# Grouped-query attention: the value products of a head pair issued in three slots in place of five

## The reference, cut to what matters

```
k_all = concatenate([cache_gqa_k, k]); v_all = concatenate([cache_gqa_v, v])
s = einsum('bqkgd,blkd->bkgql', qblk, k) * scale      # 16 heads, 4 of them share a key head
p = softmax(s)
o = einsum('bkgql,blkd->bqkgd', p, v)                 # this product
# layer 3: the latent keys of a query block are its own tile and its neighbours (+-128 tokens),
#          all 128 cached keys beside them, and one sink logit per head
```

## Time and profile before

| | |
|---|---|
| median of 3 runs | 3430.19 us |
| profiled execution | 3428.06 us |
| its span | 3426.3 us |
| TensorE matmul busy | 3130.1 us (91%) |
| VectorE busy | 2160.0 us (63%) |
| ScalarE busy | 1078.0 us (31%) |
| GpSimd busy | 318.6 us (9%) |
| mean granted TensorE clock | 0.943 of full speed |

### The profile page before, as it was taken

The page is one execution under the profiler, slowest core; times in us unless marked ns, Lnnn a source line. Parts: engine busy times, 40 slices in busy tenths (PEclk is TensorE's granted clock), DMA queues, the critical chain, the costliest instruction groups (busy, mean ns, idle before and its releaser), DMA issues.

```text
span 3426.3 us, 54082 instructions
## 1 busy us (share of the span) xinstructions
PE 3130.1 (91%) x21137; PEld 2844.0 (83%) x21137; DVE 2160.0 (63%) x4376; ACT 1078.0 (31%) x2031; POOL 318.6 (9%) x330
## 2 busy tenths in 40 slices
PE   4599999988888999998999889999998789899998
PEld 2499999966568999997775589999996657899998
DVE  5866666666656666665736646666666564666665
ACT  2232222234543222222325423222223463322221
POOL 0000000022310000000317600000002221000000
PEclk6699999989999999998998889999998899999999
DMA  7433323210022332321210033332321001222221
GB/s 290 173 116 118 114 94 118 103 33 27 1 76 97 111 122 93 115 110 54 74 52 6 4 123 121 113 122 88 120 99 39 22 1 63 69 72 71 73 72 43
DMA packets 44624, 292.27 MB, mean 85 GB/s; under 512 B 4944, under 2 KB 8272, under 8 KB 10192
## 3 DMA queue, kind: packets, MB, share of 16 engines
q1 hardware_dynamic: 44496, 290.56, 23.1%
HBM read 286.33 MB, written 4.21 MB: 85 GB/s over the span
## 4 chain that ended last, share of the span: by engine, by line
PE 83%; DVE 9%; issue 4%; ACT 3%; DMA 1%; POOL 0%; SPq 0%; POOLq 0%; DVEq 0%; ACTq 0%
PE psA L1538 37%; PE psB L1538 23%; PE psA L1653 3%; PE psA L1655 3%; PE psA L1654 3%; PE psB L1554 2%; PE psA L737 2%; PE psB L672 1%; PE psB L654 1%; ACT probs L876 1%; DVE top L1164 1%; PE psB L1561 1%; DMA m_stage<-w_mod_dram 1%; PE psB L795 1%; DVE sq_sum L1931 1%
## 5 line engine op out<-in xcount | busy, mean ns | idle before, releaser
L1538 PE MATMUL psA<-h_hi,w_hi 128*128 128x322 f32 x2816 | 655.9, 314 | 13.2 <-DVE h_lo L1971 13.2
L1538 PE MATMUL psA<-h_lo,w_hi 128*128 128x322 f32 x2816 | 652.9, 313 | 0.0
L1538 PE MATMUL psA<-h_hi,w_lo 128*128 128x322 f32 x2816 | 649.2, 312 | 0.0
L1990 DVE SCALAR_TENSOR_TENSOR xT<-psB,mod,xT 128x128 f32<-128x128 f32 x1128 | 425.8, 434 | 258.4 <-PE psB L1538 258.4
L1538 PEld LDWEIGHTS psA<-h_hi,w_hi 128*128 128x128 f32 x2816 | 477.5, 191 | 15.4 <-issue 15.2
L1538 PEld LDWEIGHTS psA<-h_lo,w_hi 128*128 128x128 f32 x2816 | 480.2, 190 | 0.0
L1538 PEld LDWEIGHTS psA<-h_hi,w_lo 128*128 128x128 f32 x2816 | 479.8, 190 | 0.0
L2047 DVE TENSOR_SCALAR conv<-u_raw,vec_sb 128x642 f32<-128x642 f32 x176 | 108.3, 615 | 486.7 <-ACT u_raw L1850 486.7
L1850 ACT ACTIVATE u_raw<-psA 128x644 f32<-128x644 f32 x176 | 124.6, 708 | 761.5 <-PE psA L1538 761.5
L1538 PE MATMUL psB<-g_hi,wo_hi 128*128 128x322 f32 x1408 | 336.3, 321 | 23.7 <-DVE g_lo L2068 23.7
L1896 DVE TENSOR_TENSOR w_lo<-w_stage,w_hi 128x512 fp32r<-128x512 f32 x504 | 321.4, 684 | 29.2 <-ACT w_hi L1764 29.1
(11 more groups left out here) (215 smaller groups left out, 4649.1 us busy)
## 6 DMA issues: line engine op xcount, KB each, us to landing
w_stage<-weights_dram SPq DMA_DIRECT2D x126, 1024.0 KB, 4.8
m_stage<-w_mod_dram SPq DMA_DIRECT2D x96, 1024.0 KB, 7.6
wo_stage<-w_out_dram SPq DMA_DIRECT2D x44, 1024.0 KB, 4.8
xT<-xT_dram SPq DMA_DIRECT2D x1, 2576.0 KB, 16.7
yT_dram<-xT SPq DMA_DIRECT2D x8, 322.0 KB, 2.2
inv_count<-inv_count_dram SPq DMA_DIRECT2D x1, 1280.0 KB, 13.6
rope_raw<-rope_dram SPq DMA_DIRECT2D x3, 256.0 KB, 2.6
k_cache_d<-ck_dram SPq DMA_DIRECT2D x8, 64.0 KB, 2.0
```

Source lines behind the costliest of these rows:

```text
L1538: ins = pe.matmul(o, wp, xp[:, a:b], start=first and n == 0, stop=last and n == 2)
L1990: ins = dve.scalar_tensor_tensor(out=xT[:, d, c:c + w], in0=psB[:, bank, at_:at_ + w], scalar=gate[:, d, i:i + 1], in1=xT[:, d, c:c + w], ...
```

## The change

The table now names tuples of key tiles: the cached tile with tile 1 in the first slot, tiles 2 and 3 two slots later, tile 4 two slots after that. The first and the last slot of a pair are the same as before. `pv` loops over the tiles that it is given; waits, matmuls, their operands and the one semaphore increment at the end are the same. ACT and DVE ask for the last tile of the tuple, and find `out_hi` and `out_lo` in the slot where they were. The new `pv` is one line longer, so L672 is L673 in the changed file, and the lines behind move with it.

```
         for d in range(KT):
-            for i, kt in enumerate((CACHE_TILE, 1, 2, 3, 4)):
-                PV_PARTS[UNIT_AT[2 * d + 1, NT - 1] + 4 + i] = (d, kt)
+            for i, kts in enumerate(((CACHE_TILE, 1), (2, 3), (4,))):
+                PV_PARTS[UNIT_AT[2 * d + 1, NT - 1] + 4 + 2 * i] = (d, kts)
...
-            def pv(d, kt):
-
-                if kt == CACHE_TILE:
+            def pv(d, kts):
+
+                if kts[0] == CACHE_TILE:
                     for h in (2 * d, 2 * d + 1):
                         g_taken(pe, l, "pc", h, 1)
                         g_taken(pe, l, "p", h, NT - 1)
                     if d:
                         pe.wait_ge(s_att[l], d)
-                qs = [j for j in range(1, NT) if kt == CACHE_TILE or l == 1 or kt in band_tiles(j)]
-                x, y = (qs[0] - 1) * P, qs[-1] * P
-                for odd in range(2):
-                    ins = pe.matmul(OUT_LAT[odd * DH:(odd + 1) * DH, x:y], value(kt, 2 * d // GROUP),
-                                    pt[(2 * d + odd) % 4][:, kt - 1, x:y], start=(kt == CACHE_TILE),
-                                    stop=(kt == NT - 1), skip_group_check=True)
-                if kt == NT - 1:
+                for kt in kts:
+                    qs = [j for j in range(1, NT) if kt == CACHE_TILE or l == 1 or kt in band_tiles(j)]
+                    x, y = (qs[0] - 1) * P, qs[-1] * P
+                    for odd in range(2):
+                        ins = pe.matmul(OUT_LAT[odd * DH:(odd + 1) * DH, x:y], value(kt, 2 * d // GROUP),
+                                        pt[(2 * d + odd) % 4][:, kt - 1, x:y], start=(kt == CACHE_TILE),
+                                        stop=(kt == NT - 1), skip_group_check=True)
+                if kts[-1] == NT - 1:
                     ins.then_inc(s_pv[l], 1)
...
-                if s - 1 in PV_PARTS and PV_PARTS[s - 1][1] == NT - 1:
+                if s - 1 in PV_PARTS and PV_PARTS[s - 1][1][-1] == NT - 1:
                     out_hi(PV_PARTS[s - 1][0])
```

## The result

The changed kernel is slower, as forecast: a median of 3446.33 us (3444.27 to 3450.71, 5 runs) against 3429.26 (3428.54 to 3431.15, 5 runs) on the same chip, a ratio of 1.0050 [1.0035, 1.0065]. The medians differ by 17.07 us. Between the profiled executions the difference is 3446.61 - 3428.06 = 18.55 us; the steps of the forecast gave 13.5.

A forecast was written before the change was run, and what follows sets the result against it. The prediction took waits on ACT's copies, released by the previous slot's scores, to bound slots with products. Its terms, 6.9 + 0.9 + 4.3 + 1.4 = 13.5 us, on the median 3430.19 gave 3443.7 us; range 3433 to 3451.

The forecast's parts named there:

- the steps of the forecast: Both attentions: first and second pairs of layers 1 and 3 lose 6.9 + 0.9 + 4.3 + 1.4 = 13.5 us.
- What bounds it: Slots with products: in every second slot TensorE waits for ACT's copy, released by scores issued one slot earlier.
- A product costs 1.19 alone and 0.86 behind another: TensorE's time per key tile in layer 1, in us; merging saves 0.33 us of TensorE's own time each.
- First pairs: Slots 12 to 16 of a group: +1.72 us for each of four in layer 1, +1.07 in layer 3.
- idle before L654: TensorE's wait for ACT's copies in slots 14 and 16: grows from 0.34 and 0.27 us to about 1.5 each.
- Second pairs of layer 1: From slot 20: DVE's work covers most of the delay; about 0.3 us is left each, 0.9 for three.
- The cover: Slot 21, layer 1: transposes already wait 0.77 us for DVE, so slot 20's extra 0.86 us end about there.
- Second pairs of layer 3: DVE covers 0.21 us of slot 20's 0.43; with slot 22's product, 0.45 us each, 1.4 for three.
- rival 4: TensorE's clock falls more often behind new gaps: up to 1.7 us each, six more, 3453.9 us; chance 0.06.
- counter-argument: Against more clock falls: slots without products, 67% busy, kept the full clock at 854 to 862 us.
- Outside the attentions the span was to be unmoved: Only the attentions of layers 1 and 3 end later, by 8 and 6 us; all else is unmoved.

The follow-up runs named there:

- the doubles in odd slots: Against the kernel before: first pairs have the cached tile in slot 12, tiles 1 and 2 in 13, 3 and 4 in 15; median 3432.92 us, ratio 1.0009.
- the doubles in 12 and 15: Against the kernel before: first pairs have the cached tile and tile 1 in slot 12, tiles 2 and 3 in 15, 4 in 16; median 3428.99 us.
- the filled kernel: The changed kernel plus throw-away matmuls of constants in layer 3's thin slots (18, 19 of each group, 61, 62); median 3441.91 us, ratio 1.0036.
- the kernel without tiles 1 and 3: The kernel before, with the products of key tiles 1 and 3 left out for pairs 0 to 6 in layers 1 and 3; 3433.11 us, one execution.
- the repetition: The changed kernel run once more with nothing edited, for a second profile; median 3444.02 us in 4 runs, ratio 1.0047.

## Why the prediction was right

**What bounds it.** Right, and shown: removing tile 1's product changed nothing past one maximum, and removing tile 2's took 0.85 us. But the loop is one of two. Scores issued in slot s release, through maximum, shift and exponential, the copy with which ACT begins its next slot; slot s+1's transposes wait for it, and slot s+1's product stands behind that wait and ahead of the scores of slot s+2. So products of even slots load one loop and those of odd slots another, and the one with more load sets the pace. Before, the even loop held three products, 2 x 0.86 + 1.19 = 2.91 us (two of them share their switch of array halves with the key transposes in slots 12 and 14), the odd one 2 x 1.19 = 2.38. The change put all five, 2.91 + 2 x 0.86 = 4.63, into the even loop: +1.72. The prediction had the first half of this, which is all that the change needed. It said that ACT copies odd tiles only and that the waits stand in even slots alone; ACT also copies the cached keys' transposes, and the wait for those in slot 17 is the odd loop's. The second half cost the prediction nothing here, and made the expectation for the doubles in odd slots wrong by some 13 us: 10 less forecast, 2.8 more measured. The count of products gives the direction of the runs with moved doubles and not their size: by it the doubles in 12 and 15 leave the even loop at 2.91 and would cost nothing, and cost 0.56.

**A product costs 1.19 alone and 0.86 behind another.** Right for its purpose: each merge costs 0.82 or 0.83 us by itself and the two 1.69. The difference of 0.33 us shows again in the product of slot 14, whose removal gave 0.86 back and not 1.19: it has transposes of keys beside it that also use half of the columns, where the prediction took all else to use the full array. That the difference is the price of entering and leaving half of the array is argued from these numbers. The Trainium skill (TensorEngine Tiling (Array Packing), Key Properties) says that a change of mode drains TensorE. The double product's 1.88 us, against 2 x 1.08 for two single ones, agrees; it never reached the sum, since TensorE had that time idle.

**First pairs.** 1.72 forecast, 1.71 to 1.72 measured in layer 1, slot by slot as worked out (slot 13 +0.82, 15 +1.69, 17 +1.69); 1.07 against 1.09 in layer 3. One sign came out differently: idle before L654 grew to 1.54 us in slot 14, as said, but in slot 16 it stayed at 0.27. The new wait on the second key's copy, 1.04 us ahead of slot 16's scores, has taken the time that TensorE would have idled before its transposes.

**Second pairs of layer 1.** 0.3 forecast, 0.49, 0.48 and 0.16 measured, the last one mixed with a fall of the clock elsewhere. The cover was DVE's, as said; 0.2 us less of it than estimated. These rows of the second pair answer to the earlier trace rows:

```profile
867.89 0.66 PE L654 MATMUL psB<-ident_sb,probs 128*128 128x128 f32 x4 [0.33 <-DVE pt L1214]
...
870.21 0.66 PE L654 MATMUL psB<-ident_sb,probs 128*128 128x128 f32 x4 [0.97 <-ACT pt L825]
...
875.29 0.66 PE L654 MATMUL psB<-ident_sb,probs 128*128 128x128 f32 x4 [0.63 <-DVE ptc L1209]
```

Slot 21's wait on DVE is 0.33 us where it was 0.77, slot 22 has a new one of 0.97 us, for ACT, and slot 24 one of 0.63 us for DVE's copy of the context unit, the one that the prediction named.

**Second pairs of layer 3: the term that was off.** "I take 0.45", 1.4 us for three; measured 6.2. The steps themselves cost 0.21 to 0.25 each, half of the estimate, as the filled kernel shows; the other 1.7 to 1.9 us each are the clock, which the sum put at nothing. It falls earlier against the context unit's scores than before, and mostly stays at 1.2 GHz for 6.9 us in place of 3.5. That is rival 4 in kind. Its price holds ("up to 1.7 us" for 3.4 us; falls of that length cost 0.0 to 1.6 here), its places don't. It looked for falls after the new gaps of slots 14 and 16, and the clock is 1.00 there in layer 1; the cost came behind slots that had a fall already. Nor does its counter-argument stand: slots 67% busy kept the full clock in its row, but 5.36 us of 7.30 did not in the kernel without tiles 1 and 3.

The account: layer 1 7.9 us; layer 3 4 x 1.09 + 3 x 0.23 = 5.1 for the steps, which makes 13.0 against 13.5 forecast; and the other 5.5 us of layer 3, the clock's. Together 18.5 of 18.55 measured. Outside the attentions the span was to be unmoved, and it is +1.35 us ahead of layer 1 and -1.15 between the layers: that sign failed, and the two nearly cancel by luck, as the falls in slots 46 and 63 of layer 3 do. So the mechanism and the steps were right, and a term of 5.5 us was missing. The forecast median, 3443.7, lies 2.6 us under the measured one, but part of that closeness is the kernel before, 0.9 us faster here than where the forecast started: between medians the loss is 17.07 us here and 15.62 in the repetition, against 13.5.

The Trainium skill (Perfetto Trace Analysis, Matmul Optimizations) says that the engine scales its power with its use and that matmuls should run back to back in batches. This case shows the other side: batches leave gaps, and the stretch at the lower clock in the first second pair of layer 3 grew from 3.5 to 6.9 us.

**Open.** Where in the slots a fall begins goes with its cost; why it begins sooner after the change, and mostly lasts twice as long, is not settled: the busy time ahead of it is the same (4.04 and 4.05 us of 6.70). The filling removes it, and doesn't say which gap matters. Nor did a run take the half-array switch alone.

## What to carry to other kernels

In a software pipeline, don't read "TensorE is 99% busy" as "TensorE is the bound": take each wait, find which earlier slot's work releases it, and count the load of every such loop, since in one that skips slots the even and the odd slots are different loops and work must be spread over both. A merge that saves switches between array halves is worth its saving only in the loop that sets the pace. And after any change that makes gaps, price the clock as well as the steps, from the stretches that are already low in the trace of before: here it was 30% of the loss between the two profiled executions.

## What the hardware showed that was not expected

- The same thin stretch can be followed by a fall or by none. Without two of five products TensorE was busy 5.36 of 7.30 us, and its clock then went to 0.50 for 6.8 us; before, in the same slots, it was busy 5.29 of 7.25 us and the clock stayed at 1.00. So less work took longer in that trace: both attentions ended later than before (0.33 and 0.79 us), though no step in them was slower.
- Adding matmuls that compute nothing took 5.5 us off the second pairs of layer 3 in the changed kernel, by the clock alone. By the end of the layer's last product, where the clock is low in that trace, 1.5 us were left of it.
- The same fall costs very different amounts. At slot 63 of the kernel before 3.4 us at the lower level cost 1.54 us. At the context unit as much cost 1.45 us when it began 1.0 us behind the last maximum ahead of it, 0.50 at 2.0 us and 0.03 at 2.55 us, where DVE had its scores already.
- At the lower level the product of a tile takes 1.98 us for four records of 512 columns, against 1.08 at full clock: 1.8 times.

```profile
2752.93 1.98 PE L673 MATMUL psB<-pt,v_cache 128*64 128x512 f32 x4
```
